# Picks of x and of the context's second tile placed seven pairs apart among the modulation chunks

## The reference, cut to what matters

```
scores = einsum('bthpd,hpkd->bthpk', qr, subkeys)
s1, i1 = top_k(scores[..., 0, :], 16);  s2, i2 = top_k(scores[..., 1, :], 16)
cand = s1[..., :, None] + s2[..., None, :]          # 256 candidates of a head
top, pos = top_k(cand, 16);  eidx = take_along_axis(cidx, pos);  gate = softmax(top)
act = gelu(einsum('ted,td->te', u[ek], hk))         # u rows: 1024 numbers
y   = einsum('te,ted->td', gk * act, v[ek])         # v rows: 1024 numbers
```

## Time and profile before

| | us |
|---|---|
| median of three runs | 3911.57 |
| profiled execution | 3919.09 |
| its span, first to last instruction | 3917.3 |
| of it pairs 80 to 207 | 898.20 to 1795.80 |
| pairs 102 to 150, with modulation chunks | 1042.40 to 1424.30 |

### The profile page before, as it was taken

How to read it: one execution, slowest core, us unless ns; L and a number is a source line. 1 busy time by engine, 2 the same in 40 slices (tenths; PEclk the granted TensorE clock), 3 DMA queues, 4 the chain that set the end, 5 groups by cost and what they waited for, 6 DMA issues and landing times.

```text
span 3917.3 us, 31941 instructions
## 1 busy us (share of the span) xinstructions
PE 2878.9 (73%) x10786; PEld 1677.7 (43%) x10786; DVE 2708.4 (69%) x5373; ACT 758.5 (19%) x1527; POOL 944.0 (24%) x795
## 2 busy tenths in 40 slices
PE   7988599667888875577986767765573097988698
PEld 2856277224322222133753434111121064967496
DVE  2556978787766689667787577767988855545453
ACT  1311121111100011111112111000011144633162
POOL 0002223233333333333332033223345300000000
PEclk9999799878999987887987878886686598999899
DMA  7349799899999998999996389989999841554154
GB/s 256 129 162 360 306 346 386 324 376 368 389 384 393 383 354 330 370 359 356 357 399 249 124 339 363 364 345 382 350 356 411 310 156 55 202 189 162 43 183 140
DMA packets 277116, 1156.47 MB, mean 295 GB/s; under 512 B 19143, under 2 KB 19784, under 8 KB 178216
## 3 DMA queue, kind: packets, MB, share of 16 engines
q0 software_dynamic: 112784, 812.33, 52.4%
q1 hardware_dynamic: 162584, 336.37, 23.6%
q10 hardware_dynamic: 1600, 5.96, 0.4%
HBM read 1150.46 MB, written 4.13 MB: 295 GB/s over the span
## 4 chain that ended last, share of the span: by engine, by line
PE 42%; DVE 28%; DMA 23%; issue 3%; ACT 3%; SPq 1%; POOL 1%; DVEq 0%; POOLq 0%; ACTq 0%; PEldq 0%
DMA arena<-in_peer_uv,arena 10%; DVE arena L2542 9%; DMA ring<-in_w_mod 9%; PE ps L1171 7%; PE ps L781 5%; DVE arena L2566 5%; PE ps L783 5%; PE ps L782 4%; PE ps L1088 4%; PE ps L900 4%; PE ps L1011 2%; PE ps L886 1%; PE ps L1135 1%; PE ps L1250 1%; DMA ring<-in_w_mlp_out 1%
## 5 line engine op out<-in xcount | busy, mean ns | idle before, releaser
L2832 POOL DMA_INDIRECT arena<-in_peer_uv,arena x768 | 929.8, 1211 | 2155.0 <-PE ps L1171 950.9
L1171 PE MATMUL ps<-arena 128*128 128x512 f32 x1664 | 982.3, 729 | 483.3 <-DVE arena L2552 469.9
L1171 PEld LDWEIGHTS ps<-arena 128*128 128x128 f32 x1664 | 349.4, 225 | 1042.0 <-DVE arena L2552 651.4
L2542 DVE CUSTOM_DVE_ANT_0 arena<-arena,hA 128x1024 f32<-128x1024 f32 x512 | 614.8, 1221 | 204.7 <-DMA arena<-in_peer_uv,arena 200.2
L1724 ACT ACTIVATE arena<-arena 128x1 f32<-128x1 f32 x768 | 155.0, 203 | 2222.0 <-DVE arena L2542 2219.2
L2566 DVE SCALAR_TENSOR_TENSOR arena<-arena 128x1024 f32<-128x1024 f32 x345 | 441.3, 1279 | 3.9 <-DVE arena L2554 0.3
L2542 DVE CUSTOM_DVE_ANT_0 arena<-arena,hB 128x1024 f32<-128x1024 f32 x256 | 308.5, 1221 | 193.9 <-DMA arena<-in_peer_uv,arena 192.3
L2073 DVE TENSOR_TENSOR w_lo<-ring,w_hi 128x1024 fp32r<-128x1024 f32 x220 | 265.2, 1223 | 180.3 <-ACT w_hi L1503 174.3
L900 PE MATMUL ps<-ring,condS 128*2 128x512 f32 x576 | 283.4, 638 | 128.7 <-DMA ring<-in_w_mod 126.4
L781 PE MATMUL ps<-hT_hi,w_hi 128*128 128x256 f32 x992 | 286.6, 289 | 17.1 <-DVE hT_lo L2081 15.3
L783 PE MATMUL ps<-hT_hi,w_lo 128*128 128x256 f32 x992 | 283.5, 286 | 0.0
(11 more groups left out here) (324 smaller groups left out, 3422.9 us busy)
## 6 DMA issues: line engine op xcount, KB each, us to landing
ring<-in_w_mod SPq DMA_DIRECT2D x48, 2048.0 KB
ring<-in_w_in SPq DMA_DIRECT2D x16, 2048.0 KB
ring<-in_w_mlp_in SPq DMA_DIRECT2D x64, 512.0 KB, 4.7
ring<-in_w_mlp_out SPq DMA_DIRECT2D x64, 512.0 KB, 5.8
ring<-in_peer_wq SPq DMA_DIRECT2D x12, 2048.0 KB
ring<-in_w_in SPq DMA_DIRECT2D x44, 512.0 KB, 5.7
ring<-in_w_out SPq DMA_DIRECT2D x6, 2048.0 KB
arena<-in_peer_uv,arena POOLq DMA_INDIRECT x768
```

The costliest lines, as they stand in the source:

```text
L1171: mm = pe.matmul(ps[:, 6 + c, :], uv[:, j % SLOTS, 0:P], uv[:, j % SLOTS, D + c * CW:D + (c + 1) * CW], start=start, stop=stop)
L2542: dve.tensor_tensor_reduce(row, row, peer_buf[p][:, t, :], 1.0, 0.0, ALU.mult, ALU.add, dots[:, column(j):column(j) + 1]).then_inc(dot_don ...
L2832: pool.indirect_dma_start(uv[:, j % SLOTS, :], None, A["peer_uv"], at).then_inc(uv_full[j % SLOTS], 16)
```

## The change

Only the two tables of pairs are changed. x's picks from the third on move from 98, 109, 120, 131, 142, 153 to 95, 104, 111, 118, 125, 132 and the three of the context from 160, 165, 170 to 139, 146, 153. No instruction is added or removed, apart from one load of an ACT table.

```
-        for k, at in zip(PICK_ORDER[5:13], (70, 87, 98, 109, 120, 131, 142, 153)):
+        for k, at in zip(PICK_ORDER[5:13], (70, 87, 95, 104, 111, 118, 125, 132)):
             PICK_SLOTS[k] = [at + i for i in range(5)]
-        for k, at in zip(PICK_ORDER[13:16], (160, 165, 170)):
+        for k, at in zip(PICK_ORDER[13:16], (139, 146, 153)):
```

## The result

The changed kernel takes 3888.18 us (median of six runs, 3882.88 to 3894.73) against 3909.29 us before (median of six, 3898.86 to 3918.6): a ratio of 0.9948, 95% interval 0.9929 to 0.9968. That is 21 us less (12 to 28 by the interval), where 15 were forecast. The profiled execution took 3894.45 us against 3919.09, span 3892.7 against 3917.3.

What follows compares the result with a forecast made beforehand. No engine always bounds: the DMA does under the modulation, DVE in pairs 151 to 175, where picks cost some 7 us. Terms -21 + 4 + 2 = -15 us off the 3911.6 median gave about 3897 us, range 3875 to 3920.

Steps and rivals of the forecast that it cites:

- the filters' rival: DVE's 14.9 us wait for the filters' tables is gained on top: -30 us, 3882 us; chance 0.25.
- Picks out of the stretch that DVE bounds: Picks 160, 165, 170 leave their windows, whose 15 pairs then go at 5.61 us each: 21.0 us less.
- Seven picks under the modulation: Pairs 102 to 150: seven picks start in pairs 104 to 146 instead of four, hidden by DMA transfers: 4 us more.
- Pick 98 to 95: The pick moves away from the first chunks' transfers, to a lower DMA share: 2 us more, 2.9 at worst.
- The reload: Held scores reload between modulation traffic, needed by DVE two pairs later: taken as nothing, 6 us if slow.
- Bias additions behind the pieces: Where a pick's piece and a bias addition share a pair, the store comes some 5 us later, but this hides.
- the ring's sign: PE's waits for chunks over 90 us, or pairs 102 to 150 over 400 us, would prove the forecast wrong.
- The filters' wait: DVE's 14.9 us wait for the filters' tables goes, counted as nothing since transfers bound that window, share 1.02.
- The ring's rival: Chunk ring sets the pace in pairs 102 to 150: 39.1 us more there, 3932 us in all; chance 0.12.
- its mark of 370: In pairs 102 to 150, a rate under 370 GB/s, 19 us more, decides against the change.
- The late gathers' rival: Gathers issued too late under denser picks cost 15 us, taking back the gain: 3911 us; chance 0.15.

Runs made afterwards that it cites:

- filters_late: Kernel before the change, with the filters' first piece at pair 184 in place of 176, picks unmoved: 3907.34 us, ratio 0.9996.
- load_late: Changed kernel, with SP issuing the filters' tables, norm's rows and two weight chunks only after PE added pair 174's rows: 3890.79 us, ratio 0.9946.
- nopick_before: Kernel before the change, without the work of the context's picks 160, 165 and 170: 3890.33 us, ratio 0.9945.
- nopick_after: Changed kernel, without the work of the context's same three picks, there at pairs 139, 146 and 153: 3884.33 us, ratio 0.9929 to before.
- light: Kernels before and after the change, loading a quarter of each chunk of the second to fourth modulation matrix: 3792.21 and 3772.3 us.
- bare: Kernels before and after the change, with no load of the second to fourth modulation matrix: 3780.81 and 3756.8 us.
- Tight: Kernel before, with x's picks at 70, 87, 102, 107, 112, 118, 123, 128 and the context's three at 135, 140, 145: 3880.73 us, ratio 0.9924.
- after: The changed kernel itself, against the kernel before: 3888.18 us, ratio 0.9948.
- light_after: Changed kernel, loading a quarter of each chunk of the second to fourth modulation matrix: 3772.3 us, ratio 0.9658 to before.
- bare_after: Changed kernel, with no load of the second to fourth modulation matrix: 3756.8 us, ratio 0.9588 to before.
- x_only: Kernel before, with only x's picks moved as in the change and the context's three left at 160, 165, 170: 3907.98 us, ratio 0.9995.

## Why the prediction was right, and where its terms were off

The direction, the place and the size were right; the time, 3888.18, lies at the lower end of the forecast's own range (3888 to 3905), and nearer to the 3882 of the filters' rival than to the likeliest 3897. So the time alone would not decide between the two; filters_late and load_late do. The gain is 21 us against 15. Of the signs that the prediction named, pairs 158 to 175 took 113.4 us at a share of 1.01 (about 121 were forecast), pairs 176 to 183 42.6 (45), pairs 102 to 150 391.4 at 0.97 (386 at 0.96), and the filters' wait is gone.

1. Picks out of the stretch that DVE bounds, -21 us. Measured -23.0 (nopick_before), 19 by the medians. Right. The pace of 5.61 us a pair was a little slow: without picks pairs 158 to 175 took 96.5 / 18 = 5.36 us each.
2. Seven picks under the modulation, +4 us. The stretch grew by 9.5 us, more than twice the term, and by some 8.5 us' worth of bytes, of which 2.1 MB (5.4 us) are the next point's. 8.0 of the 9.5 are there without the context's picks (nopick_after, 389.9 us), and their two add 1.5. The term was too small, and the reasoning incomplete. I named the transfers as the cover and nothing else, and on that built the expectations of the light and bare runs, which failed. PE's work is a second cover below it, and it was to be seen in the earlier trace rows: PE busy for 33 to 39 of the 42 to 50 us.
3. Pick 98 to 95, +2 us. Pairs 87 to 101 took 101.4 us at 343 GB/s and a share of 0.89, 34.8 MB, against 100.6 us at 367 GB/s and 0.94, 36.9 MB, before. With the 2.1 MB that these pairs now leave to the next stretch (5.4 us at 388 GB/s) the cost is nearer 6 us than 2: this term was too small. In these pairs pick 87 and all of pick 95 stand now, where four of pick 98's five pieces stood. Tight, which has only pick 87 there, needs 96.8.
4. The reload, nothing. It was issued at 1326.3, landed within 9.2 us instead of 6.0, and nothing of DVE waits for it at pair 139: the only wait there is 1.55 us for a gather. Right.
5. Bias additions behind the pieces, nothing. PE's waits for chunks stayed (61.1 us against 62.0), far from the 90 that would have been the ring's sign. Right.
6. The filters' wait, nothing. filters_late (ratio 0.9996) and load_late, which has a wait of 20.7 us and the full gain, both say so. Right, and the wait's rival is refuted.

Between the 15 us forecast and the measured 21 (runs) to 25 (profile) lie 6 to 10 us. By the profile, pairs 158 to 183 gave 26.6 us where 21 were forecast, and pairs 87 to 150 took 10.3 where 6 were. For two more stretches the prediction had nothing. Pairs 151 to 157 gave 4.3 us: they took 41.9 to 45.4 us in the four kernels with the changed picks (after, load_late, light_after, bare_after) and 47.0 to 49.3 in the six with the former ones and pick 153. Why stays open. And 4.4 lie in pairs 192 to 207, where all the kernels with the filters at 176 were faster than the one before, so that this may be chance in the one profile of before.

The ring's rival: the stretch stayed at 387 GB/s, above its mark of 370. The late gathers' rival: GpSimd's time per issue did rise (15.16 us for 11 at pick 104), in a window whose DMA share is 1.00, so it is not on the path, as with the earlier trace rows. Nor do the rows show that a pick as such lengthens an issue: in the windows of picks 160 and 170 it took 1.30 and 0.93 us.

## What to carry to other kernels

Work that can be moved costs little only where another engine or the DMA has more to do in the same steps of the pipeline. With few buffers that must hold for every stretch of a few steps, and in this kernel spreading the work out was no substitute: list the stretches by what bounds them (the DMA share beside each engine's busy time), and put the movable work where something else is the bound. Here steps of five pairs still worked. A wait that the trace shows, in a stretch that transfers bound, is worth only as much as the DMA engines idle in it: here they were at a share of 1.02, and removing it brought nothing.

## What was not expected of the hardware

Gathers ran at 396 to 399 GB/s in pairs 158 to 175 with almost nothing else to move (nopick_before, load_late), above the 379 to 388 GB/s of the earlier trace rows; and at 424 GB/s in the five pairs 153 to 157 of x_only, right after the last chunk. And leaving out 25 MB x 3 of chunk loads shortened the kernel by only 139 us (3919.99 to 3780.81 beside each other), less than the 195 us that 75.5 MB take at 388 GB/s. Pairs 102 to 150 shrank by 66 us, from 381.9 to 315.8, and PE was then busy for 307 of these.
